# One-hots times gates moved from GpSimd to VectorE, and the next tile's query work dealt out over the placement batches

## The chip, the cores and the metric

One core of a Trainium2 chip runs the program alone. The metric is the device time of one execution in microseconds. Before the change three runs gave 3329.55, 3333.01 and 3342.83 us, median 3333.01.

## What is computed

One layer of a streaming encoder for 1024 prompt tokens and 8 x 16 sample tokens, so 9 tiles of 128 tokens with 1024 features. Two mixers and a projection come first; then each token asks for experts, and this is where the change lies:

```python
q = (h @ wq).reshape(N, 8, 2, 128)
s = einsum('nhpc,hpkc->nhpk', q, keys)          # 128 keys per head and half
sv, si = top_k(s, 16)                           # 16 best of 128, twice per head
cv, ci = top_k(sv[:, :, 0, :, None] + sv[:, :, 1, None, :], 16)   # 16 best pairs
expert = i1 * 128 + i2                          # the two keys of each pair
gate = softmax(cv)
a = gelu(einsum('nd,nhkd->nhk', h, u[expert]))
out = einsum('nhk,nhkd->nd', gate * a, v[expert])
```

Each token has 8 heads x 16 = 128 slots, each with two keys (below 128) and a gate. There are 16384 experts.

## The kernel before, in words

The program has four stages: modulation, mixing, routing, experts. Four of the nine tiles fetch the rows of their experts one by one ("picked" tiles); the other five are computed against the whole expert table ("dense" tiles), and for them the routing writes a matrix of gates per token, 128 x 128 keys, to memory. The change touches `routing` alone.

**Periods.** `periods` (L764) goes over the tiles in the order 0, 1, 4, 5, 6, 7, 8, 2, 3 (L761). Each engine runs the same sequence of periods, each with three parts for three tiles: *choose* (VectorE's search for the best keys of a tile), *done* (the tile chosen before it is indexed if it is picked, or placed if it is dense) and *prepare* (query product and scores of the tile that comes next). Periods 3 to 7 place the five dense tiles; 0, 1, 2 and 8 place nothing. In period 1 VectorE also does 32 dot products for tile 0 (`use`, L1088), whose rows GpSimd fetches (`fetch`, L830).

**Placement** of a tile goes in 16 batches of 8 tokens. For each, VectorE compares the slots' keys with a counter and makes two one-hots of 128 slots by 128 keys by 8 tokens in bf16 (`hot_rows`, L1105: left_hot L1113, right_hot L1116, stored with the 8 tokens innermost). ScalarE turns left_hot into f32 `left`, token by token (`left_rows`, L904). GpSimd multiplies right_hot by the gate into f32 `right`, also token by token (`place` on GpSimd, L839, instruction L846). TensorE multiplies right by left for each token (`place`, L1192), and ScalarE copies the result into `dense` (`take_gates`, L911). SP stores half a tile at a time (`store`, L802) behind its load of a coming tile's h2T (`load_h2`, L797), which waits for that query product's end. All of left_hot, right_hot, left and right have two buffers: one-hots of batch b wait for the reader of batch b - 2, right and left wait for the placement of batch b - 2 (`wait_for_placed`, L757).

**Query work** of VectorE for one tile: `two_lists` (L968) takes 16 maxima of 8, 16 pairs of index and replace, 16 maxima, 16 indices; `best_pairs` (L996) the same over the sums; `chosen_ranks` (L1029) the arithmetic on ranks, the product of hit with key_wide twice (L1066, L1070) and the sums; `softmax` (L1095) the gates. `own.settle()` waits for all of VectorE's own results so far; the call `rows(b)` ahead of most of them puts batch b of the placement there, so that the wait is filled. `rows(0)` stands behind the 16 pairs of index and replace. ScalarE makes key_wide (`widen_keys`, L893) and the exponential.

**Preparation** on TensorE: `product` (L1153) is one of four column blocks of the query product, 8 steps each (two matmul records per step); ScalarE copies it (`take_q`, L866), TensorE turns it (`turn`, L1171), ScalarE copies that (`take_qT`, L872), and `scores` (L1174) follows. In a period TensorE does product 0 first, then turns the slots of the tile done (`turn_slots`, L1182, which waits for the gates), product 1 with a turn in it, and then per batch the placement and two steps of products 2 and 3.

Which batch issues what is written out by hand in the engines' `period` functions; all engines run in program order.

Of the kernel before, what the change touches and what calls it, by code (L numbers as in the profile page):

```python
# [8 lines left out]
ALU = mybir.AluOpType  # L9
# [3 lines left out]
P = 128  # L13
D = 1024
KD = D // P
# [12 lines left out]
NKEYS = 128  # L28
# [669 lines left out]
def routing(nc, ctx, wq, keys, u_table, v_table, ident_in, shared, h2_rows, h2T_tiles, gate_blocks, picks):  # L698
# [12 lines left out]
    with ExitStack() as mem:  # L711
# [59 lines left out]

        def picks_rows(n):

            return ORDER[n] < PICKED
# [49 lines left out]
        def _(pool):  # L824
# [14 lines left out]
            def place(t):  # L839

                d = t - FIRST_DENSE
                pool.wait_ge(S.slotsT, t * 2 + 2)
                for b in range(BATCHES):
                    wait_for_placed(pool, d, b)
                    pool.wait_ge(S.right_hot, d * BATCHES + b + 1)
                    nc.gpsimd.tensor_tensor(  # L846
                        right[b % 2][:, :, :], right_hot[b % 2][:, :, :].rearrange("p i t -> p t i"),
                        gateT[:, b * BATCH:(b + 1) * BATCH].rearrange("p (t o) -> p t o", o=1)
                        .to_broadcast([P, BATCH, NKEYS]), ALU.mult).then_inc(S.right, 1)

            def period(choose, done, prepare):
                indexed, placed = split(done)
                if placed is not None:
                    place(placed)
# [3 lines left out]
            periods(period)  # L858

        @block.scalar  # L860
        def _(act):
# [59 lines left out]
            def period(choose, done, prepare):  # L921
                indexed, placed = split(done)
                if prepare is not None:
                    take_q(prepare, 0)
# [4 lines left out]
                if prepare is not None:  # L929
                    take_qT(prepare, 0)  # L930
                    take_q(prepare, 1)
                for b in range(BATCHES):
# [4 lines left out]
                    if prepare is not None and b in (4, 8):  # L937
                        take_q(prepare, b // 4 + 1)
                    if prepare is not None and b in (1, 5, 9):
                        take_qT(prepare, b // 4 + 1)  # L940
                    if choose is not None and b == 6:
                        widen_keys(choose, 0)
                    if choose is not None and b == 12:
                        act.wait_ge(S.shifted, choose + 1)
                        nc.scalar.activation(soft[:, :, :], soft[:, :, :], ACT.Exp).then_inc(S.exp, 1)
                    if choose is not None and b == 14:
                        widen_keys(choose, 1)
# [8 lines left out]
        def _(dve):  # L956
# [11 lines left out]
            def two_lists(t, rows):  # L968

                for n in range(HP):  # L970
# [3 lines left out]
                    own.mark(nc.vector.max(best[:, n, low], s_ps[:, n, :]))  # L974
                own.settle()
# [4 lines left out]
                rows(0)  # L980
# [4 lines left out]
                rows(1)  # L985
# [4 lines left out]
                rows(2)  # L990
# [3 lines left out]
                rows(3)  # L994
# [1016 lines left out]
```

## Time and profile before

| what | us |
|---|---|
| median of three runs | 3333.01 |
| profiled execution | 3337.24 |
| its span | 3335.6 |
| TensorE matmul busy | 3045.6 (91%) |
| VectorE busy | 2407.0 (72%) |
| GpSimd busy | 1489.0 (45%) |
| ScalarE busy | 935.2 (28%) |
| routing, from the first to the last of its query work | 512.6 to 1183.6 |
| placement, first left_hot to last dense copy | 724.8 to 1138.5 |

The span is the time from the first to the last instruction of the one profiled execution. Busy shares are means over stages that are bound by different engines; the routing stage is a fifth of the span and is read for itself. In the rows further down, PE is TensorE, DVE VectorE, ACT ScalarE, POOL GpSimd; L numbers are lines of the kernel; a group's row has the output and inputs, the shapes, the number of instructions, the busy time, the mean ns of one, and the idle time of the engine before them with what ended it. `work` is the memory of both the sums and hit; the names `shared` and `wq_sb` are the query weights.

### The profile page before, as it was taken

The page shows a single profiled execution, that of the slowest core. Times are in us where ns is not written, and L with a number is a line of the kernel's source. Part 1 is how long each engine was busy: PE and PEld are TensorE (multiplying, and loading weights), DVE is VectorE, ACT ScalarE, POOL GpSimd, SP SyncE. Part 2 cuts the span into 40 slices and gives each one's busy share as a digit, 9 for nine tenths or more (in the row PEclk, how much of TensorE's full clock was granted, in tenths as well). Part 3 has the DMA queues.
Part 4 walks back from the last instruction along what each step waited for, and adds up shares of the span by engine and source line. Part 5 has one row for each costly group of instructions (what it writes and reads, how often), then busy time and mean ns, then how long its engine had stood idle before and what let it go on. Part 6 is the DMA issues. An engine that isn't in the chain of part 4 may idle for free.

```text
span 3335.6 us, 43974 instructions
## 1 busy us (share of the span) xinstructions
PE 3045.6 (91%) x16658; PEld 2331.2 (70%) x16658; DVE 2407.0 (72%) x4987; ACT 935.2 (28%) x1271; POOL 1489.0 (45%) x1188
## 2 busy tenths in 40 slices
PE   8899978577888469999999999999999999999997
PEld 1466644245555369988888887888888888788886
DVE  1233324999988878887777777878777777778798
ACT  0111111138888622222222222222122222212222
POOL 0010000425554334346656565656565565666453
PEclk9999989889999879999999999999999999999999
DMA  9711131602222367789999999999999999999883
GB/s 357 212 64 63 57 145 64 208 7 108 108 108 108 151 223 264 265 292 353 366 351 366 359 350 368 353 370 353 355 351 369 349 360 344 352 347 336 307 295 140
DMA packets 305919, 858.73 MB, mean 257 GB/s; under 512 B 25376, under 2 KB 108832, under 8 KB 303984
## 3 DMA queue, kind: packets, MB, share of 16 engines
q0 software_dynamic: 151344, 551.09, 45.1%
q1 hardware_dynamic: 154333, 305.79, 25.6%
q8 instruction: 64, 1.05, 0.1%
q14 instruction: 70, 0.57, 0.1%
q10 hardware_dynamic: 108, 0.22, 0.0%
HBM read 793.86 MB, written 63.15 MB: 257 GB/s over the span
## 4 chain that ended last, share of the span: by engine, by line
PE 50%; DMA 5%; POOL 4%; DVE 3%; issue 2%; ACT 0%; DVEq 0%; SPq 0%; ACTq 0%
PE y_ps L1889 22%; PE a_ps L1870 20%; PE picked_ps L1907 5%; DMA shared<-in_peer_u,ids 3%; PE uT_ps L1857 3%; POOL shared L1453 2%; POOL quad L1464 1%; DMA shared<-in_peer_v,ids 1%; DVE uT_lo L1615 1%; DVE shared L1674 1%; DVE shared L1644 0%; DMA quad<-in_peer_v,idsT 0%; DVE shared L1657 0%; ACT uT_hi L1534 0%; DVE m_lo L1630 0%
## 5 line engine op out<-in xcount | busy, mean ns | idle before, releaser
L1453 POOL DMA_INDIRECT shared<-in_peer_u,ids x480 | 560.7, 1168 | 595.3 <-DVE acts L1657 507.1
L1657 DVE CUSTOM_DVE_ANT_0 shared<-shared 128x1024 f32<-128x1024 f32 x480 | 579.2, 1221 | 173.5 <-DMA shared<-in_peer_u,ids 172.9
L1870 PE MATMUL a_ps<-h_hi,uT_lo 128*128 128x320 f32 x2048 | 643.8, 314 | 1.7 <-DVE h_lo L1786 1.7
L1870 PE MATMUL a_ps<-h_hi,uT_hi 128*128 128x320 f32 x2048 | 633.8, 309 | 0.0
L1870 PE MATMUL a_ps<-h_lo,uT_hi 128*128 128x320 f32 x2048 | 633.8, 309 | 0.0
L1889 PE MATMUL y_ps<-v_hi,m_lo 128*128 128x512 f32 x1280 | 511.5, 400 | 25.7 <-DVE shared L1644 14.6
L1644 DVE TENSOR_TENSOR shared<-shared,y_ps 128x512 f32<-128x512 f32 x630 | 422.5, 685 | 150.2 <-PE y_ps L1889 149.5
L1889 PE MATMUL y_ps<-v_lo,m_hi 128*128 128x512 f32 x1280 | 504.6, 394 | 0.0
L1889 PE MATMUL y_ps<-v_hi,m_hi 128*128 128x512 f32 x1280 | 502.3, 392 | 0.0
L1464 POOL DMA_INDIRECT quad<-in_peer_v,idsT x384 | 443.9, 1156 | 120.1 <-issue 120.1
L1870 PEld LDWEIGHTS a_ps<-h_hi,uT_lo 128*128 128x128 f32 x2048 | 386.1, 189 | 7.2 <-issue 2.1
L1870 PEld LDWEIGHTS a_ps<-h_lo,uT_hi 128*128 128x128 f32 x2048 | 386.2, 189 | 4.9
L1870 PEld LDWEIGHTS a_ps<-h_hi,uT_hi 128*128 128x128 f32 x2048 | 385.5, 188 | 0.0
L1543 ACT ACTIVATE m_all<-a_ps 128x320 f32<-128x320 f32 x256 | 112.1, 438 | 918.2 <-PE a_ps L1870 918.2
L846 POOL TENSOR_TENSOR right<-right_hot,gateT 128x1024 f32<-128x1024 bf16 x80 | 215.6, 2698 | 264.6 <-DVE right_hot L1116 203.0
L1889 PEld LDWEIGHTS y_ps<-v_hi,m_lo 128*128 128x128 f32 x1280 | 241.2, 188 | 117.0 <-issue 33.6
L1889 PEld LDWEIGHTS y_ps<-v_hi,m_hi 128*128 128x128 f32 x1280 | 241.7, 189 | 53.9
L1534 ACT ACTIVATE uT_hi<-uT_ps 128x512 fp32r<-128x512 f32 x254 | 138.0, 596 | 488.7 <-PE uT_ps L1857 488.7
L1889 PEld LDWEIGHTS y_ps<-v_lo,m_hi 128*128 128x128 f32 x1280 | 241.8, 189 | 40.3
L1200 PE MATMUL place_ps<-left,right 128*128 128x128 f32 x1280 | 171.6, 290 | 87.8 <-ACT dense L918 64.8
L1200 PEld LDWEIGHTS place_ps<-left,right 128*128 128x128 f32 x1280 | 158.7, 202 | 120.9 <-issue 107.0
L1453 POOL DMA_INDIRECT shared<-in_peer_v,ids x128 | 154.2, 1205 | 186.8 <-DVE shared L1674 155.2
(187 smaller groups left out, 4197.2 us busy)
## 6 DMA issues: line engine op xcount, KB each, us to landing
shared<-in_peer_u SPq DMA_DIRECT2D x128, 512.0 KB, 7.5
v_all<-in_peer_v SPq DMA_DIRECT2D x128, 512.0 KB, 7.5
gate_blocks<-dense SPq DMA_DIRECT2D x10, 4096.0 KB, 12.1
gates<-gate_blocks SPq DMA_DIRECT2D x64, 640.0 KB, 22.1
w_ada<-in_w_ada SPq DMA_DIRECT2D x12, 2048.0 KB, 11.7
x_in<-in_x_prompt SPq DMA_DIRECT2D x16, 512.0 KB, 4.5
shared<-in_peer_u,ids POOLq DMA_INDIRECT x480, 8.7
shared<-in_w_in SPq DMA_DIRECT2D x8, 768.0 KB, 13.2
```

The source lines that it names most:

```text
L846: nc.gpsimd.tensor_tensor(right[b % 2][:, :, :], right_hot[b % 2][:, :, :].rearrange("p i t -> p t i"), gateT[:, b * BATCH:(b + 1) * BATCH ...
L1200: last = nc.tensor.matmul(place_ps[:, g, j, :], right[b % 2][:, g * 4 + j, :], left[b % 2][:, g * 4 + j, :], start=True, stop=True)
L1453: pool.indirect_dma_start(out=rows[n % 4], out_offset=None, in_=u_table if n < DOTS else v_table, in_offset=bass.IndirectOffsetOnAxis(ap=i ...
L1464: pool.indirect_dma_start(out=quads[half][q], out_offset=None, in_=v_table, in_offset=bass.IndirectOffsetOnAxis(ap=idsT[:, t, token:token ...
L1534: nc.scalar.activation(uT_hi[s][:, n * 4:n * 4 + 4, :], uT_ps[:, n * 4:n * 4 + 4, :], ACT.Copy)\
L1543: nc.scalar.activation(m_all[j][parity][:, n * GROUP:(n + 1) * GROUP], a_ps[n][:, 0:GROUP], ACT.Gelu).then_inc(S.gelu, 1)
L1644: nc.vector.tensor_tensor(part, part, y_ps[n % RING][:, :], ALU.add).then_inc(S.y_free, 1)
L1657: nc.vector.tensor_tensor_reduce(out=rows[n % 4], in0=rows[n % 4], in1=token_row, scale=1.0, scalar=0.0, op0=ALU.mult, op1=ALU.add, accum_ ...
L1857: last = nc.tensor.transpose(uT_ps[:, k, :], u[s][:, k * P:(k + 1) * P], ident[:, :])
L1870: last = nc.tensor.matmul(a_ps[n][:, 0:GROUP], lhs[s][:, k, :], rhs[:, k, tok], start=k == 0 and m == 0, stop=k == KD - 1 and m == 2)
L1889: last = nc.tensor.matmul(y_ps[n % RING][:, :], lhs[j][parity][:, tok], rhs[j][parity][:, col], start=j == 0 and m == 0, stop=j == 1 and m ...
L1907: last = nc.tensor.matmul(picked_ps[n][q * 32:(q + 1) * 32, :], spread[:, half, q, :], quads[half][q][:, n * HALF:(n + 1) * HALF], start=o ...
```

## The change

- GpSimd's placement loop goes. VectorE multiplies right_hot by the gate itself, in `hot_rows`, behind a wait for its own right_hot and for the placement of the batch before last.
- The calls of `rows` move: batch 0 behind the first 16 maxima, batches 1 to 5 among the 16 pairs of index and replace, batch 6 in the middle of the second maxima, 7 to 9 among the indices, 10 to 15 at the waits of `best_pairs` and `chosen_ranks`; none later.
- TensorE turns the slots first, and deals the four products out over batches 0 to 11 (3, 3 and 2 steps each), with turns in batches 4, 7, 10, 13 and scores in 9, 10, 12, 15. ScalarE's copies follow (`take_q` in 2, 5, 8, 11, `take_qT` in 5, 8, 11, 14), key_wide in 11 and 15.

```diff
+        QUERY_ENDS, SCORED = (2, 5, 8, 11), (9, 10, 12, 15)
...
-            def place(t):
-
-                d = t - FIRST_DENSE
-                pool.wait_ge(S.slotsT, t * 2 + 2)
-                for b in range(BATCHES):
-                    wait_for_placed(pool, d, b)
-                    pool.wait_ge(S.right_hot, d * BATCHES + b + 1)
-                    nc.gpsimd.tensor_tensor(
-                        right[b % 2][:, :, :], right_hot[b % 2][:, :, :].rearrange("p i t -> p t i"),
-                        gateT[:, b * BATCH:(b + 1) * BATCH].rearrange("p (t o) -> p t o", o=1)
-                        .to_broadcast([P, BATCH, NKEYS]), ALU.mult).then_inc(S.right, 1)
...
-            periods(period)
...
@@ ScalarE, period @@
-                if prepare is not None:
-                    take_q(prepare, 0)
                 if indexed is not None:
                     take_index(indexed)
                 if placed is not None:
                     take_slots(placed)
-                if prepare is not None:
-                    take_qT(prepare, 0)
-                    take_q(prepare, 1)
                 for b in range(BATCHES):
...
-                    if prepare is not None and b in (4, 8):
-                        take_q(prepare, b // 4 + 1)
-                    if prepare is not None and b in (1, 5, 9):
-                        take_qT(prepare, b // 4 + 1)
-                    if choose is not None and b == 6:
+                    if prepare is not None and b in QUERY_ENDS:
+                        take_q(prepare, QUERY_ENDS.index(b))
+                    if prepare is not None and b - 3 in QUERY_ENDS:
+                        take_qT(prepare, QUERY_ENDS.index(b - 3))
+                    if choose is not None and b == 11:
                         widen_keys(choose, 0)
-                    if choose is not None and b == 12:
+                    if choose is not None and b == 15:
                         act.wait_ge(S.shifted, choose + 1)
                         nc.scalar.activation(soft[:, :, :], soft[:, :, :], ACT.Exp).then_inc(S.exp, 1)
-                    if choose is not None and b == 14:
                         widen_keys(choose, 1)
@@ VectorE, two_lists @@
                     own.mark(nc.vector.max(best[:, n, low], s_ps[:, n, :]))
+                rows(0)
                 own.settle()
...
-                rows(0)
+                    if n % 3 == 2:
+                        rows(1 + n // 3)
                 own.settle()
...
@@ VectorE, hot_rows @@
-                wait(dve, S.right, d * BATCHES + max(b - 1, 0))
+                if b > 1 or d:
+                    dve.wait_ge(S.right, d * BATCHES + b - 1)
                 nc.vector.tensor_tensor(right_hot[b % 2][:, :, :], key(1), keys_iota, ALU.is_equal)\
                     .then_inc(S.right_hot, 1)
+                wait_for_placed(dve, d, b)
+                dve.wait_ge(S.right_hot, d * BATCHES + b + 1)
+                nc.vector.tensor_tensor(
+                    right[b % 2][:, :, :], right_hot[b % 2][:, :, :].rearrange("p i t -> p t i"),
+                    gateT[:, b * BATCH:(b + 1) * BATCH].rearrange("p (t o) -> p t o", o=1)
+                    .to_broadcast([P, BATCH, NKEYS]), ALU.mult).then_inc(S.right, 1)
@@ TensorE, period @@
-                if prepare is not None:
-                    product(prepare, 0)
                 if done is not None:
                     turn_slots(done)
-                if prepare is not None:
-                    product(prepare, 1, range(0, 5))
-                    if done is not None:
-                        pe.wait_ge(S.slotsT, done * 2 + 2)
-                    turn(prepare, 0)
-                    product(prepare, 1, range(5, KD))
                 for b in range(BATCHES):
                     if placed is not None:
                         place(placed - FIRST_DENSE, b)
-                    if prepare is not None:
-                        if b < 8:
-                            product(prepare, 2 + b // 4, range(b % 4 * 2, b % 4 * 2 + 2))
-                        if b in (0, 4, 8):
-                            turn(prepare, b // 4 + 1)
-                        if b in range(9, 13):
-                            scores(prepare, b - 9)
+                    if prepare is None:
+                        continue
+                    if b - 2 in QUERY_ENDS:
+                        if b - 2 == QUERY_ENDS[0] and done is not None:
+                            pe.wait_ge(S.slotsT, done * 2 + 2)
+                        turn(prepare, QUERY_ENDS.index(b - 2))
+                    if b <= QUERY_ENDS[-1]:
+                        product(prepare, b // 3, range(b % 3 * 3, min(b % 3 * 3 + 3, KD)))
+                    if b in SCORED:
+                        scores(prepare, SCORED.index(b))
```

## Rows read from the trace of the kernel before

**Rows 1.** table of windows: the period without placement, the five with it (busy us)

```profile
core 0: us, PE busy (x) PEld busy (x) DVE busy (x) ACT busy (x) POOL busy (x), PEclk, DMA share, GB/s
668.30:712.90 44.60, 35.55 (x114) 17.89 (x114) 40.74 (x219) 9.13 (x13) 0.00 (x0) 0.92 0.04 12
712.80:1138.30 425.50, 335.15 (x1839) 240.82 (x1839) 382.03 (x1249) 345.01 (x304) 215.64 (x80) 0.96 0.26 104
```

**Rows 2.** timeline of VectorE: the first maxima of three queries (start, duration, us)

```profile
668.34 3.26 DVE L974 MAX8 best<-s_ps 128x8 f32<-128x128 f32 x16
712.85 0.29 DVE L974 MAX8 best<-s_ps 128x8 f32<-128x128 f32 x1
1138.28 0.49 DVE L974 MAX8 best<-s_ps 128x8 f32<-128x128 f32 x2
```

**Rows 3.** groups by line, VectorE, 712.8 to 1138.3 (busy us, mean ns, idle before)

```profile
L1113 DVE TENSOR_TENSOR left_hot<-keyT,iota_keys 128x1024 bf16<-128x1024 bf16 x80 | 113.1, 1414 | 32.0 <-ACT left L908 31.9
L1116 DVE TENSOR_TENSOR right_hot<-keyT,iota_keys 128x1024 bf16<-128x1024 bf16 x80 | 65.5, 819 | 2.3 <-POOL right L846 2.3
L1066 DVE TENSOR_TENSOR work<-work,key_wide 128x2048 bf16<-128x2048 bf16 x5 | 16.7, 3344 | 0.2
L1070 DVE TENSOR_TENSOR work<-work,key_wide 128x2048 bf16<-128x2048 bf16 x5 | 11.2, 2240 | 6.8 <-ACT key_wide L900 6.8
```

**Rows 4.** groups by line, ScalarE, 712.8 to 1138.3

```profile
L908 ACT ACTIVATE left<-left_hot 128x1024 f32<-128x1024 bf16 x80 | 171.6, 2150 | 4.6 <-DVE left_hot L1113 4.6
L918 ACT ACTIVATE dense<-place_ps 128x512 f32<-128x512 f32 x160 | 163.3, 1152 | 8.1 <-PE place_ps L1200 8.0
```

**Rows 5.** timeline of VectorE: the first batch's one-hots, GpSimd idle

```profile
724.75 0.68 DVE L1113 TENSOR_TENSOR left_hot<-keyT,iota_keys 128x1024 bf16<-128x1024 bf16 x1
725.35 0.68 DVE L1116 TENSOR_TENSOR right_hot<-keyT,iota_keys 128x1024 bf16<-128x1024 bf16 x1
```

**Rows 6.** timeline of VectorE in the period without placement

```profile
700.54 0.43 DVE L1041 TENSOR_TENSOR ranks<-digits 128x256 f32<-128x256 uint32 x1
701.00 0.42 DVE L1044 TENSOR_TENSOR ranks<-ranks,narrow 128x256 f32<-128x256 f32 x1
707.97 1.22 DVE L1070 TENSOR_TENSOR work<-work,key_wide 128x2048 bf16<-128x2048 bf16 x1 [2.04 <-ACT key_wide L900]
```

**Rows 7.** groups by line, shapes apart, whole span: operands in order or broadcast

```profile
L546 DVE TENSOR_TENSOR x_in<-x_in,gated_mix 128x1024 f32<-128x1024 f32 x9 | 11.0, 1226 | 0.7
L412 ACT ACTIVATE squares<-x_in 128x1024 bf16<-128x1024 f32 x9 | 9.4, 1049 | 119.2 <-DMA x_in<-in_x_prompt 119.2
L1003 DVE TENSOR_TENSOR work<-best 128x512 f32<-128x512 f32 x9 | 6.2, 685 | 0.0
```

**Rows 8.** timeline of TensorE: second placement period, and the first placement of all

```profile
836.27 2.00 PE L1200 MATMUL place_ps<-left,right 128*128 128x128 f32 x16
838.11 1.88 PE L1162 MATMUL q_ps<-wq_sb,h2T 128*128 128x512 f32 x4
728.66 3.75 PE L1200 MATMUL place_ps<-left,right 128*128 128x128 f32 x16 [6.24 <-issue]
```

**Rows 9.** timeline of ScalarE, VectorE and TensorE in the periods 0 and 2

```profile
580.19 0.60 ACT L870 ACTIVATE q<-q_ps 128x512 f32<-128x512 f32 x1 [2.76 <-PE q_ps L1162]
581.33 3.74 PE L1179 MATMUL s_ps<-keysT,qT 128*128 128x128 f32 x32
582.18 1.22 DVE L1066 TENSOR_TENSOR work<-work,key_wide 128x2048 bf16<-128x2048 bf16 x1
694.43 0.60 ACT L870 ACTIVATE q<-q_ps 128x512 f32<-128x512 f32 x1 [2.76 <-PE q_ps L1162]
```

**Rows 10.** timeline at the start of period 1; landing times of line 834

```profile
591.05 3.26 DVE L974 MAX8 best<-s_ps 128x8 f32<-128x128 f32 x16
590.66 1.04 POOL L834 DMA_INDIRECT dense<-in_peer_u,ids  x1 [88.29 <-DVE ids L1085]
DMA to landing us min/median/max: 4.3/5.8/8.2
```

More of the change, by code:

```diff
@@ L837, in fetch @@
                     .then_inc(row_loaded[slot % 8], 16)
-            def place(t):
-                d = t - FIRST_DENSE
-                pool.wait_ge(S.slotsT, t * 2 + 2)
-                for b in range(BATCHES):
-                    wait_for_placed(pool, d, b)
-                    pool.wait_ge(S.right_hot, d * BATCHES + b + 1)
-                    nc.gpsimd.tensor_tensor(
-                        right[b % 2][:, :, :], right_hot[b % 2][:, :, :].rearrange("p i t -> p t i"),
-                        gateT[:, b * BATCH:(b + 1) * BATCH].rearrange("p (t o) -> p t o", o=1)
-                        .to_broadcast([P, BATCH, NKEYS]), ALU.mult).then_inc(S.right, 1)
[L851 to L854, printed above, removed]
             pool.wait_ge(S.picked, 1)
@@ L984, in two_lists @@
                     own.mark(nc.vector.max(best[:, n, high], work3[:, n, :]))
-                rows(1)
+                    if n == 7:
+                        rows(6)
                 own.settle()
@@ L989, in two_lists @@
                     own.mark(nc.vector.max_index(best_at[:, n, high], best[:, n, high], work3[:, n, :]))
-                rows(2)
+                    if n in (3, 9, 15):
+                        rows(7 + n // 6)
                 own.settle()
@@ L993, in two_lists @@
                 nc.vector.tensor_copy(best_key[:, :, :], best_at[:, :, :]).then_inc(S.best_key, 1)
-                rows(3)
             def best_pairs(t, rows):
@@ L1007, in best_pairs @@
                         ALU.add))
-                rows(4)
                 own.settle()
@@ L1013, in best_pairs @@
                         own.mark(nc.vector.max(pair[:, h, part], sums[:, h]))
-                    rows(5 + n * 3)
+                    rows(10 if part is low else 13)
                     own.settle()
@@ L1018, in best_pairs @@
                         own.mark(nc.vector.max_index(pair_at[:, h, part], pair[:, h, part], sums[:, h]))
-                    rows(6 + n * 3)
+                    rows(11 if part is low else 14)
                     own.settle()
@@ L1024, in best_pairs @@
                             own.mark(nc.vector.match_replace(sums[:, h], pair[:, h, low], sums[:, h], NEG))
-                        rows(7)
+                        rows(12)
                         own.settle()
@@ L1038, in chosen_ranks @@
                 own.mark(nc.vector.tensor_scalar(narrow[:, :, :], pair_at[:, :, :], NW, None, ALU.is_ge))
-                rows(10)
+                rows(15)
                 own.settle()
                 own.mark(nc.vector.tensor_tensor(ranks[:, :], digits[:, 2:4], digits[:, 0:2], ALU.subtract))
-                rows(11)
                 own.settle()
@@ L1046, in chosen_ranks @@
                     .to_broadcast([P, 2, HEADS, TOPK]), ALU.mult))
-                rows(12)
                 own.settle()
                 own.mark(nc.vector.tensor_tensor(ranks[:, :], ranks[:, :], digits[:, 0:2], ALU.add))
-                rows(13)
                 own.settle()
@@ L1055, in chosen_ranks @@
                 own.mark(nc.vector.tensor_copy(rank[:, 1], ranks[:, 1]))
-                rows(14)
                 own.settle()
@@ L1067, in chosen_ranks @@
                     .then_inc(S.first_keyed, 1)
-                rows(15)
                 dve.wait_ge(S.key_wide, t * 2 + 2)
```

## The prediction, made before the changed kernel was run

> **What bounds the kernel now.** I read the page's engine shares and its chain of waits first. The chain is TensorE's in the expert stage, and nothing of the change lies there, so the question is one stage only: the routing, whose placement periods are read with the table of windows [rows 1]. Five periods place a dense tile each; from the first maximum of one query to that of the next they last 425.4 us together (712.85 to 1138.28), 85.1 us each [rows 2]. One period without placement, the query of one tile alone, lasts 44.5 us (668.34 to 712.85) [rows 2]. Everything after the routing waits for it, so what a period gains or loses goes into the total one to one.
>
> In the placement window VectorE is busy 382 of 425.5 us, 90%; ScalarE 345, TensorE 335, GpSimd 216 [rows 1]. The reader should see that GpSimd, the engine that the change empties, has the most room, and VectorE, which gets its work, the least. VectorE's own idle time is mostly left_hot waiting for ScalarE, 31.9 us [rows 3]. So the first half of a period is VectorE's and the second ScalarE's: there it does left and two dense copies per batch, 171.6 + 163.3 us for 80 batches, 4.2 us each by the records, which overlap a little [rows 4].
>
> The row that argues for the change: left_hot takes 0.68 us where GpSimd is idle [rows 5] but 1.41 us in the mean, right_hot 0.82, and the two multiplications of hit by key_wide, of one form, 3.34 and 2.24 us in these periods [rows 3] against 1.22 without GpSimd [rows 6]. GpSimd's multiplication slows VectorE.
>
> **The change part by part.**
>
> *Removed.* 80 multiplications, 216 us in all [rows 1], leave GpSimd. They had no time of their own on the path, since VectorE and ScalarE set it. What returns is VectorE's: 80 x (1.41 - 0.68) + 80 x (0.82 - 0.68) + 5 x (3.34 - 1.22) + 5 x (2.24 - 1.22) = 58 + 11 + 11 + 5 = 85 us of busy time; some of it was hidden behind the wait for ScalarE.
>
> *Added.* 80 multiplications on VectorE, 128x1024, f32 out. The trace shows none with this operand order: right_hot is stored key by key with the 8 tokens innermost and is read token by token, so each bf16 element lies 16 bytes from the one before it. Bounds: below, the f32 product of 128x1024 with operands in order, 1.23 us [rows 7]; 0.68 us, right_hot's own time with bf16 in and out, would need the speed of bf16, and I hold it unlikely because gate and output are f32. Above, ScalarE's pair of rows: 1.05 us for 128x1024 in order [rows 7], 2.15 us for left [rows 4], the very same turned read of a one-hot; the ratio 2.05 on 1.23 gives 2.5 us. The broadcast gate costs nothing (sums of two broadcast operands, 128x512, 0.685 us [rows 7], about half of 1.23). I take the nearest row, ScalarE's turned read, and its extra 1.0 to 1.1 us as a time rather than a ratio, rounded down: m = 2.2 us.
>
> One batch on VectorE is then left_hot 0.60 (start to start [rows 5]), right_hot 0.68, a wait on its own result of 0.03 (an operation that waits starts 0.03 us behind the end of its producer, 700.97 to 701.00 [rows 6]), and m less the 0.08 us by which the next starts early: 3.43 us. Behind the new waits (own result, placement of the batch before last) stands the whole query chain of the next tile.
>
> *Moved query work on VectorE.* The hot rows go to other places between the same instructions; the count stays 16. Eight of the groups still stand directly ahead of a wait for VectorE's own results and fill it. A bare wait costs some 0.2 us (0.03 behind the end in place of 0.08 to 0.09 before it, plus the lost overlap of the short ones), so the chain of 44.5 us loses 8 x 0.2 = 1.6 us.
>
> *A placement period after the change:* 44.5 - 1.6 + 16 x 3.43 = 97.8 us if VectorE is never held up, against 85.1: +12.7 us, five times +63.5 us. The way of summing holds for the kernel before: the same sum with its rows, 44.5 + 16 x (1.41 + 0.82 - 0.16) + 3.1 for the hit products + 34/5 of waits for left and right [rows 3] - 16 x 0.2, gives 84.3 where 85.1 was measured.
>
> *What must keep up.* ScalarE has 345/5 = 69 us of work per period, 98 us to do it in. TensorE's new batch holds three steps of a query product in place of two: place 1.84 us (836.27 to 838.11), steps of 0.86 (two of them, four records of 0.43 us, in the 1.88 us row with its last overlap taken off), so 4.4 us, with a turn 4.9 [rows 8]; VectorE's batch in the first third, with three pairs of index and replace at 0.53 us (16 of them between the maxima's 3.4 us behind 712.85 and left_hot at 724.75 [rows 2, 5]), is 3.43 + 1.6 = 5.0. It just keeps up, and two buffers of right and left take the rest. Turning the slots ahead of the first product frees the tile edge, and rows(0) goes out right behind the 3.26 us of maxima [rows 2], not 8.5 us later. That spread is a gain for ScalarE and TensorE, and I cost it at nothing because VectorE's chain covers it.
>
> *Moved queue work.* No DMA is added. SP's load of h2T waits for the last product, now in batch 11 instead of 7; it and the store of half a tile queued behind it have four batches of some 5 us and the tail of the query as cover, so nothing; without the cover each period would lose what reaches past its end. GpSimd's queue keeps only its early fetches.
>
> *Periods without placement*, where the new order costs. Period 0: two of the four groups of scores (3.74 us in all, so 1 each) now come before the last product's end, so ScalarE's last take_q moves from 580.19 to 582.2; the first key_wide, about 1.9 us (VectorE waits 2.04 for the second [rows 6]), now queues behind it and is done at 584.6, where VectorE wants it at 582.18: 2.4, and with the exponential that also queues behind it +3 us [rows 9]. Period 1: rows(0) moves to 3.3 us behind the first maximum at 591.05, but the first row was asked for at 590.66 and takes 4.3 to 8.2 us: +3 [rows 10]. Period 2: TensorE does all four products in the period, not three: 16 records of 0.43 us and a wait of 0.7 more, so with the scores the last take_q moves from 694.43 to 704.0, and key_wide is done at 706.4, where VectorE wants it at 704.7 (707.97 less the wait and one product): +2 [rows 6, 9]. Together +8 us, between 0 and 16.
>
> **Sum.** The profiled execution took 3337.2 us, its span 3335.6; 63.5 + 8 = +72 makes 3409. The median of the three runs shown is 4.2 us below it, so 3405.
>
> **Rivals.**
> 1. *The turned read costs VectorE only part of what it costs ScalarE.* For: nothing in the rows ties the two engines; ScalarE's slope may be its own. With half of the extra, m = 1.75, a batch is 2.98 and a period 90.6: 5 x 5.5 + 8 = +36, 3369. It decides by m alone; 0.25.
> The Trainium skill's Vector Engine (DVE) Microarchitecture Reference, section 5.2 (Measured stream behaviour on trn2), says that a port streams at full rate only over runs of at least two adjacent words, and gives 1.73 ns per column where one source hops at every element. An estimate from that is 1.8 us plus some 0.15 fixed, m = 1.9, and 3381 us. No run here shows it yet; it speaks against the change as my row does.
> 2. *The turned read is free on VectorE* (the other side). m = 1.23: a batch 2.46, a period 82.2, -14.5 + 8 = -6, 3327. For: no row shows VectorE paying for such a read. Against: ScalarE pays for the very same one. It decides below m = 1.5, where the total comes within 17 us; 0.11.
> 3. *Faster*: m near 1.0 or less, so that ScalarE's 69 us and the query's tail bound a period at about 78: -27, 3306; 0.07. Against: VectorE's f32 rows.
> 4. *TensorE becomes the bound.* It now idles from the last place to the next, some 20 us per tile, and after 6.2 us of idle time 16 place records took 3.75 us, not 2.00 [rows 8]. If the first twelve batches ran at such a rate (8.2 us each), a period would be about 120 us and the total 3510. Against: one batch later the records are at the quick pace again, as the table's mean over the placement shows (clock 0.96 [rows 1]); 0.02.
>
> **How the numbers follow.** My forecast (m between 1.9 and 2.5, 3381 to 3429) has 0.55, rival 1 has 0.25, rivals 2 to 4 have 0.11, 0.07 and 0.02. Slower by over 0.5% (17 us, about what a measurement can tell here) 0.82, same 0.11, faster 0.07. The range takes in the forecast and rival 1 with the bounds of m and of the periods without placement: low 3355 (m = 1.65 and nothing lost there), high 3445 (m = 2.5, twice the 8 us and as much again of waits not foreseen).
>
> **What would show it.** Multiplications on VectorE, 80 of about 2.2 us; left_hot and right_hot at 0.68 throughout; both hit products at 1.22; periods of 98 us between first maxima; VectorE over 95% busy in the placement window, with ScalarE and TensorE waiting for right and left_hot, not the reverse. I am wrong if the multiplication is near 1.23, or if periods are longer than the sum of VectorE's rows, which would put the wait on place or left.

## The result, and the profile after

The changed kernel takes 3466.88 us (median of 4 runs, 3460.10 to 3468.73), the kernel before 3337.18 (4 runs): ratio 1.0386, 95% interval [1.0358, 1.0415]. It is slower, as forecast, but by 130 us where the working said 72, and outside the range. The profiled execution took 3467.91 us, 130.7 more than that of before.

Where the time went is read first from the first maxima of each query, the rows that answer to [rows 2]. VectorE's timeline of the changed kernel, at the period without placement, the first placed one and the last (start, duration, us):

```profile
531.57 0.89 DVE L953 MAX8 best<-s_ps 128x8 f32<-128x128 f32 x4 [41.72 <-PE s_ps L1162]
596.72 3.25 DVE L953 MAX8 best<-s_ps 128x8 f32<-128x128 f32 x16
...
678.65 1.47 DVE L953 MAX8 best<-s_ps 128x8 f32<-128x128 f32 x7
...
725.36 0.89 DVE L953 MAX8 best<-s_ps 128x8 f32<-128x128 f32 x4
...
1266.52 0.69 DVE L953 MAX8 best<-s_ps 128x8 f32<-128x128 f32 x3
```

The five placed periods last 541.2 us (725.36 to 1266.52), 108.2 each, against 425.4 before: +115.7. Periods 0 to 2 last 65.15, 81.93 and 46.71 us where they had been 61.90, 77.29 and 44.51: +10.1. The first maximum comes 2.4 us later and what stands behind the placement takes 2.4 us longer. That is the whole 130.7, to the rounding. My sum had 63.5 and 8 for the first two, so 52 of the 58 us that are missing lie in the placed periods.

The table of windows over that stretch, answering to [rows 1] (busy us and instructions of each engine, granted clock, DMA share):

```profile
678.65:725.30 46.65, 36.00 (x114) 17.98 (x114) 40.55 (x218) 8.69 (x13) 0.00 (x0) 0.94 0.04 12
725.30:1266.60 541.30, 374.48 (x1855) 280.45 (x1855) 457.00 (x1329) 346.47 (x305) 0.00 (x0) 0.82 0.21 85
```

GpSimd's column is empty, as the change says. VectorE is busy 457 of 541 us, 84%, where it had been 90% before and over 95% was forecast. So VectorE has 75 us more work and is waiting more, and no other engine is near full. TensorE needs 374 us for the work that took 335, at a granted clock of 0.82 in place of 0.96. The groups by line of VectorE in the same stretch (busy us, mean ns, idle before and what ended it), answering to [rows 3, 5]:

```profile
L1097 DVE TENSOR_TENSOR right<-right_hot,gateT 128x1024 f32<-128x1024 bf16 x80 | 160.7, 2009 | 57.2 <-PE place_ps L1183 50.7 <-DVE right_hot L1093 1.4
L1093 DVE TENSOR_TENSOR right_hot<-keyT,iota_keys 128x1024 bf16<-128x1024 bf16 x80 | 54.8, 685 | 0.0
L1089 DVE TENSOR_TENSOR left_hot<-keyT,iota_keys 128x1024 bf16<-128x1024 bf16 x80 | 54.2, 678 | 12.9 <-ACT left L893 12.9
...
L1046 DVE TENSOR_TENSOR work<-work,key_wide 128x2048 bf16<-128x2048 bf16 x5 | 6.1, 1225 | 10.2 <-ACT key_wide L885 10.2
L1043 DVE TENSOR_TENSOR work<-work,key_wide 128x2048 bf16<-128x2048 bf16 x5 | 6.1, 1224 | 0.2
```

The right-hand numbers are the news: 57.2 us in which the multiplication waits, 50.7 of them for TensorE's placement, and 12.9 in which left_hot waits for ScalarE: 14 us a period. Who holds up TensorE stands in the waits of the same stretch (us in total, times, longest):

```profile
ACT q L855 <- PE q_ps L1145: 104.4, 20, 6.3
PE place_ps L1183 <- ACT dense L903: 102.1, 29, 5.9
...
DVE right L1097 <- PE place_ps L1183: 50.7, 27, 3.5
```

TensorE waits for ScalarE's dense copies 102 us, ScalarE for TensorE's query product 104 us, 20 times: once for each product. The same two lines before the change:

```profile
PE place_ps L1200 <- ACT dense L918: 64.8, 47, 3.5
...
ACT q L870 <- PE q_ps L1162: 37.2, 11, 6.9
```

TensorE waited for dense before, too, but in many short gaps; ScalarE waited for q in 11, not 20. That the two engines now wait for each other in a loop is seen in the timeline of the second placed period. TensorE:

```profile
870.02 1.95 PE L1183 MATMUL place_ps<-left,right 128*128 128x128 f32 x16
871.81 1.88 PE L1145 MATMUL q_ps<-shared,h2T 128*128 128x512 f32 x4
877.79 3.75 PE L1183 MATMUL place_ps<-left,right 128*128 128x128 f32 x16 [4.10 <-ACT dense L903]
881.33 3.70 PE L1145 MATMUL q_ps<-shared,h2T 128*128 128x512 f32 x6
884.87 1.95 PE L1183 MATMUL place_ps<-left,right 128*128 128x128 f32 x16
```

ScalarE over the same stretch:

```profile
873.73 0.60 ACT L855 ACTIVATE q<-q_ps 128x512 f32<-128x512 f32 x1 [5.44 <-PE q_ps L1145]
874.22 0.59 ACT L860 ACTIVATE qT<-x_ps 128x512 f32<-128x512 f32 x1
874.70 2.02 ACT L893 ACTIVATE left<-left_hot 128x1024 f32<-128x1024 bf16 x1
876.61 1.92 ACT L903 ACTIVATE dense<-place_ps 128x512 f32<-128x512 f32 x2
```

Read the two together. ScalarE has finished left and the copies of the batch before, and `take_q` is next in its queue. It waits 5.44 us, because TensorE ends that product only behind the placement of the same batch (870.02) and two more steps (871.81 to 873.69). What TensorE needs for its next placement, left of the next batch and the first dense copy of this one (which frees the half of place_ps), stands behind `take_q` in ScalarE's queue. So the two engines take turns: TensorE idles 4.10 us. Then it pays again: the next 16 records of the placement take 3.75 us where the others take 1.95. (The 20 such gaps of the five periods last 3.6 to 5.9 us, and the 16 records behind each take 3.4 to 3.8.) The windows around it (same columns as above) show the clock:

```profile
870.00:874.00 4.00, 3.69 (x21) 2.36 (x19) 3.86 (x18) 0.27 (x1) 0.00 (x0) 1.00 0.00 0
874.00:878.00 4.00, 0.21 (x1) 0.24 (x2) 3.90 (x12) 4.00 (x5) 0.00 (x0) 0.80 0.00 0
878.00:882.00 4.00, 4.00 (x17) 3.67 (x18) 2.19 (x8) 3.68 (x4) 0.00 (x0) 0.50 0.00 0
...
886.00:890.00 4.00, 4.00 (x22) 2.56 (x20) 3.49 (x5) 1.93 (x2) 0.00 (x0) 1.00 0.01 4
```

The granted clock goes from 1.00 (2.4 GHz) to 0.50 (1.2 GHz) in the stretch that follows the idle one, and is at 1.00 again in the window from 886 on. VectorE feels it when a `right` that needs the buffer of that batch waits for the late placement:

```profile
881.58 2.00 DVE L1097 TENSOR_TENSOR right<-right_hot,gateT 128x1024 f32<-128x1024 bf16 x1 [1.81 <-PE place_ps L1183]
```

The same picture stands at 893.37 and 913.54 (waits of 5.44 and 6.30 us), in all in batches 2, 5, 8 and 11 of every placed period.

### The profile page after: what moved, and what is told of

Same layout as the page of the kernel before. It is cut to its first block, busy times and chain, and to the rows that moved or that the text cites. A ratio compares the mean times of both kernels' runs of the same rounds, so it can differ in the third digit from the quotient of the medians.

```text
span 3466.3 us, 43971 instructions
## 1 busy us (share of the span) xinstructions
PE 3084.3 (89%) x16658; PEld 2370.6 (68%) x16658; DVE 2483.2 (72%) x5067; ACT 934.5 (27%) x1271; POOL 1271.0 (37%) x1108
## 4 chain that ended last, share of the span: by engine, by line
PE 49%; DMA 5%; POOL 3%; DVE 3%; issue 2%; ACT 0%; DVEq 0%; SPq 0%; ACTq 0%
PE y_ps L1867 22%; PE a_ps L1848 20%; PE picked_ps L1885 4%; DMA shared<-in_peer_u,ids 3%; PE uT_ps L1835 3%; POOL shared L1431 2%; POOL quad L1442 1%; DMA shared<-in_peer_v,ids 1%; DVE uT_lo L1593 1%; DVE shared L1652 0%; DVE shared L1622 0%; DVE shared L1635 0%; ACT uT_hi L1512 0%; DMA quad<-in_peer_v,idsT 0%; DVE m_all L1603 0%
## 5 line engine op out<-in xcount | busy, mean ns | idle before, releaser
L1867 PE MATMUL y_ps<-v_hi,m_lo 128*128 128x512 f32 x1280 | 512.7, 401 | 26.5 <-DVE shared L1622 14.3
L1183 PE MATMUL place_ps<-left,right 128*128 128x128 f32 x1280 | 200.9, 323 | 129.7 <-ACT dense L903 102.1
L1183 PEld LDWEIGHTS place_ps<-left,right 128*128 128x128 f32 x1280 | 192.2, 235 | 163.7 <-issue 133.9
## 6 DMA issues: line engine op xcount, KB each, us to landing
gate_blocks<-dense SPq DMA_DIRECT2D x10, 4096.0 KB, 12.9
```

Source lines behind the costliest of these rows:

```text
L1183: last = nc.tensor.matmul(place_ps[:, g, j, :], right[b % 2][:, g * 4 + j, :], left[b % 2][:, g * 4 + j, :], start=True, stop=True)
L1867: last = nc.tensor.matmul(y_ps[n % RING][:, :], lhs[j][parity][:, tok], rhs[j][parity][:, col], start=j == 0 and m == 0, stop=j == 1 and m ...
```

## The experiments

Periods are from first maximum to first maximum; a placed period is the mean of the five. Each ratio is to runs of the kernel before on the same chip; its median was 3335.65 us over the 25 of them that stand beside e5 to e8.

| run | multiplies | query work | placed period | us | ratio, 95% interval |
|---|---|---|---|---|---|
| before | GpSimd | old order | 85.1 | 3337.18 | 1 |
| after | VectorE | spread | 108.2 | 3466.88 | 1.0386 [1.0358, 1.0415] |
| e1 | VectorE | spread, q one batch later | 96.0 | 3397.21 | 1.0189 [1.0162, 1.0215] |
| e2 | GpSimd | spread | 106.5 | 3460.33 | 1.0371 [1.0349, 1.0393] |
| e3 | VectorE | old order | 92.9 | 3373.22 | 1.0116 [1.0094, 1.0139] |
| e4 | VectorE, read in stored order | as e1 | 83.5 | 3337.59 | 1.0001 [0.9988, 1.0014] |
| e5 | GpSimd | as e1 | 81.7 | 3327.34 | 0.9970 [0.9960, 0.9980] |
| e6 | VectorE, 8 tensor_scalar | as e1 | 85.2 | 3345.29 | 1.0027 [1.0016, 1.0038] |
| e7 | VectorE, 8 tensor_scalar | old order | 84.5 | 3337.32 | 1.0003 [0.9993, 1.0014] |
| e8 | VectorE | as e1 in two of four places | 101.3 | 3426.84 | 1.0265 [1.0248, 1.0282] |
| e9 | GpSimd | as e5; old order where nothing is placed | 82.2 | 3326.61 | 0.9962 [0.9946, 0.9977] |
| e10 | GpSimd | as e9, key_wide ahead of the last q | 81.9 | 3321.05 | 0.9945 [0.9930, 0.9961] |

**e1: the copy of q one batch later.** Only ScalarE's order changes:

```diff
-                    if prepare is not None and b in QUERY_ENDS:
-                        take_q(prepare, QUERY_ENDS.index(b))
+                    if prepare is not None and b - 1 in QUERY_ENDS:
+                        take_q(prepare, QUERY_ENDS.index(b - 1))
```

> The changed kernel, but ScalarE copies each finished query product one batch later (batches 3, 6, 9, 12 in place of 2, 5, 8, 11), behind left and the dense copies of that batch. Theory A (ScalarE stands at take_q until TensorE, behind the placement of the same batch, has ended the product, and left and the dense copies queue behind it): the idle time of ScalarE before take_q in the placement window falls from 120 us to under 30, VectorE's waits for the placement from 51 us to under 15, and a placement period from 108.2 us to VectorE's sum of 95 to 98 (44.5 - 1.6 + 16 x 3.23 = 94.6 and a few us of waits), so 3395 to 3415 us. Rival B (three product steps per batch are too much for TensorE, whatever ScalarE does): periods stay above 104 us and the total above 3440. Rival C (the price is the multiplication alone): unchanged, 3460 to 3470.

Measured: 3397.21 us, placed periods of 96.0. The waits for q are gone, and ScalarE now waits for VectorE, as the prediction had wanted it. Groups of ScalarE, then of VectorE, over the five placed periods of e1:

```profile
L893 ACT ACTIVATE left<-left_hot 128x1024 f32<-128x1024 bf16 x80 | 165.6, 2070 | 88.8 <-DVE left_hot L1089 88.8
...
L855 ACT ACTIVATE q<-q_ps 128x512 f32<-128x512 f32 x20 | 12.9, 643 | 0.0
```

```profile
L1097 DVE TENSOR_TENSOR right<-right_hot,gateT 128x1024 f32<-128x1024 bf16 x80 | 160.9, 2011 | 9.3 <-DVE right_hot L1093 1.4
```

The window of the five placed periods of e1 (columns as above):

```profile
720.47:1200.49 480.02, 349.64 (x1855) 253.89 (x1855) 456.56 (x1328) 349.10 (x305) 0.00 (x0) 0.88 0.24 96
```

VectorE is busy 95% of the time here, as the prediction had expected of the changed kernel. Idle time ahead of `right` and left_hot falls from 70.1 to 9.3 us, 12.2 a period, and the period falls by just that, 108.2 to 96.0. Moving one instruction by one batch gives 70 us back, 61 of them in the placed periods, so the queue order is shown to be the cause of the excess, not the multiplication's price (it is the same 2.01 us) nor GpSimd's absence.

**e8: the same in two places of four.**

```diff
-                    if prepare is not None and b in QUERY_ENDS:
+                    if prepare is not None and b in (3, 6):
+                        take_q(prepare, b // 3 - 1)
+                    if prepare is not None and b in (8, 11):
                         take_q(prepare, QUERY_ENDS.index(b))
```

> The changed kernel with only the first two of the four take_q moved one batch later. If each take_q is a stall of its own, half of the difference between the changed kernel (108.2 us per period) and e1 (96.0) comes back: 102 us, 3425 to 3440 us. If one stall is enough to hold up the whole period, 3455 or more.

Measured: 3426.84 us, periods of 101.3, near the middle of 108.2 and 96.0, and 10 waits for q (46.8 us) where there had been 20. Each early copy is a stall of its own, worth some 3 us of the period.

**e2 and e3: one part of the change each.** e2 is the changed kernel with GpSimd's loop put back (and the multiplication taken out of `hot_rows`); e3 is the kernel before with that loop taken out and the multiplication put into `hot_rows`, and nothing moved:

```diff
@@ e2, against the kernel after; e3 is the reverse, against the kernel before @@
+            def place(t):
...
+                    nc.gpsimd.tensor_tensor(
...
-                nc.vector.tensor_tensor(
-                    right[b % 2][:, :, :], right_hot[b % 2][:, :, :].rearrange("p i t -> p t i"),
```

> The changed kernel with the multiplication given back to GpSimd as it was; the dealing out of the query work and the places of the hot rows stay as changed. Theory A: four times per period ScalarE's wait for the product and TensorE's wait for left and the dense copies follow each other, about 7.6 us from one placement to the next instead of 4.4 (4 x 7.6 + 12 x 4.4 = 83, and some 10 us at the tile edge), so periods of 90 to 97 us although nothing was added to VectorE, and a total of 3370 to 3410 us, slower than before. Rival C (the multiplication on VectorE is the whole loss): as before or faster, 3340 us or less.

> The kernel before with the multiplication alone moved to VectorE; the query work and the hot rows stay where they were. Theory A: VectorE's chain sets the period, 44.5 - 3.2 + 16 x 3.23 = 93.0 us in place of 85.1, without the 10 us that the periods without placement lost: 3337 + 40 = 3377, between 3365 and 3395 us. Rival D (VectorE's new wait for the placement is what costs): periods above 100 us and 3420 us or more.

e3 came as forecast: 3373.22 us, placed periods of 92.9, and the three periods without placement at 61.84, 77.30 and 44.53, as before. e2 was a miss: the spread alone, with VectorE relieved of the multiplication, still costs 124 us (0.0371 x 3337), with periods of 106.5. I had taken the stall to be cheap where VectorE has time to spare. It isn't: VectorE is busy only 353 of e2's 532.5 us, and the period is nearly that of the kernel after, so the loop of ScalarE and TensorE holds it up by itself (e5 below takes the loop out). The waits of e2:

```profile
POOL right L848 <- PE place_ps L1194: 240.9, 62, 9.0
...
DVE left_hot L1106 <- ACT left L910: 164.6, 40, 12.5
...
ACT q L872 <- PE q_ps L1156: 110.9, 20, 6.3
PE place_ps L1194 <- ACT dense L920: 101.8, 29, 5.9
```

The last two are the pair of the kernel after, to within 7 us; GpSimd waits for the placement and VectorE for left. So the parts don't add: the spread costs 21.4 us a period with GpSimd multiplying, the multiplication 7.8 in the old order, both together 23.1. In the kernel after, the multiplication that I had priced at nearly the whole loss is all but hidden behind the loop: 108.2 against 106.5.

**e5: GpSimd multiplies, q one batch later.** e2 with the edit of e1.

> GpSimd multiplies as in the kernel before, the query work is spread as changed, and take_q comes one batch later. If the spread of the change cost only through take_q, its loss goes: VectorE's sum with GpSimd's disturbance is 44.5 - 1.6 + 16 x 2.07 + 3.1 = 79 us per period, so 79 to 84 us where the kernel before has 85.1, and with the 10 us of the periods without placement 3315 to 3345 us. If the spread costs by itself (TensorE's longer batches), periods stay above 90 us and the total above 3365.

Measured: 3327.34 us, ratio 0.9970: below both kernels, though by 0.3% only against the one before. With GpSimd multiplying, the copy one batch later takes the placed period from 106.5 to 81.7, so the early copy alone costs 24.8 us a period there. With the copy in its place the spread is a gain of 3.4 us a period, though periods 0 to 2 lose 6.8 us together. And e1 against e5 is the price of the multiplication on VectorE once the loop is out: 96.0 against 81.7, 14.3 us a period, 70 us in the total.

**e4: what the turned read costs.** e1, with right_hot read in the order in which it is stored; the gates of the dense tiles then land at other keys.

```diff
-                    right[b % 2][:, :, :], right_hot[b % 2][:, :, :].rearrange("p i t -> p t i"),
+                    right[b % 2][:, :, :], right_hot[b % 2][:, :, :].rearrange("p (t j) u -> p t (j u)", t=BATCH),
```

> As e1_q_later, but the multiplication reads right_hot in the order in which it is stored, so the one-hots times gates land at the wrong keys (the gates of the dense tiles are wrong, the work is the same). If the turned read is what makes the multiplication 2.0 us, it takes 1.2 us here; the period falls by 16 x 0.8 = 12 us against e1_q_later to 82 to 87 us (ScalarE's and TensorE's 69 us do not bound it) and the total by about 60, to 3330 to 3360. If the f32 output or the broadcast gate makes it 2.0 us, nothing changes against e1_q_later.

The group of the multiplication in e4, over its five placed periods:

```profile
L1097 DVE TENSOR_TENSOR right<-right_hot,gateT 128x1024 f32<-128x1024 bf16 x80 | 98.0, 1226 | 9.3 <-DVE right_hot L1093 0.9 <-PE place_ps L1183 0.5
```

1226 ns, to the nanosecond the f32 product in order of [rows 7], against 2011: the stride costs 0.785 us of each, 80 x 0.785 = 63 us, and the total falls by 60. This is the measured price of the operand order by itself.

**e6 and e7: no right_hot, no turned read.** Each token's row of `right` is made by one instruction from its key and gate, eight per batch; e6 on e1, e7 on the kernel before.

```diff
...
-                nc.vector.tensor_tensor(right_hot[b % 2][:, :, :], key(1), keys_iota, ALU.is_equal)\
-                    .then_inc(S.right_hot, 1)
...
+                for t in range(BATCH):
+                    tok = b * BATCH + t
+                    last = nc.vector.tensor_scalar(right[b % 2][:, t, :], iota_row[:, :], gateT[:, 0, tok:tok + 1],
+                                                   gateT[:, 1, tok:tok + 1], ALU.is_equal, ALU.mult)
...
```

> take_q one batch later, and VectorE makes right in one pass per token: eight operations of 128x128 per batch compare a row counter with the token's key and multiply by its gate, both as scalars per partition, in place of right_hot and the turned multiplication (2.75 us per batch). A 128x128 operation with a constant took 0.16 us from start to start, so 1.24 us per batch: VectorE 44.5 - 1.6 + 16 x 1.84 = 72 us per period. Theory: ScalarE's 69 us with its own waits then share the bound, 75 to 82 us per period, 3295 to 3335 us, below both kernels. If scalars from memory make an operation 0.3 us or more, 90 us and more, 3370 or above.

> As e6, but with the order of the kernel before (query work and hot rows where they were). VectorE's sum is 44.5 - 3.2 + 16 x 1.84 = 71 us. If the spread is worth something once VectorE is lighter, this is slower than e6: the tile edge stays (slots turned behind a whole product, batch 0 behind the 16 pairs), 78 to 85 us per period, 3305 to 3338 us. If it is worth nothing, this beats e6 by the 10 us of the periods without placement.

e6 missed: 3345.29 us. Eight such instructions in a row take 2.14 us, 0.27 each, where I had expected 0.155. Timeline of VectorE in e6:

```profile
762.74 0.67 DVE L1091 TENSOR_TENSOR left_hot<-keyT,iota_keys 128x1024 bf16<-128x1024 bf16 x1
763.33 2.14 DVE L1096 TENSOR_SCALAR right<-iota_row,gateT 128x128 f32<-128x128 f32 x8
```

That is more than `right` alone had cost, though right_hot (0.68) falls away. e7 lands at 3337.32, 1.0003 [0.9993, 1.0014]: taking the work off GpSimd in this way gains nothing that can be told from no change. It is 8 us below e6, as its expectation had it for a spread that is worth nothing. Most of that is the periods 0 to 2, 7.2 us together; a placed period is 0.7 us shorter. With the turned multiplication, e3 with its periods of 92.9 is below e1 with 96.0. So once q is copied late, the old order is no worse for a VectorE that multiplies, and better by 3.1 us a period with the dearer multiplication. That fits its groups of work, which stand ahead of more of the waits for VectorE's own results, but the two orders differ in more than that, and it wasn't tried apart.

**e9 and e10: the periods without placement.** e9 is e5 with the old order of TensorE, ScalarE and the dot products wherever no tile is placed; but key_wide stood behind the last copy of q. e10 puts it ahead:

```diff
@@ e10, against e9 @@
-                    for b in range(4 if prepare is not None else 0):
-                        take_qT(prepare, b)
-                        if b < 3:
+                    for b in range(4):
+                        if prepare is not None:
+                            take_qT(prepare, b)
+                        if choose is not None and b == 2:
+                            widen_keys(choose, 0)
+                        if prepare is not None and b < 3:
                             take_q(prepare, b + 1)
                     if choose is not None:
-                        widen_keys(choose, 0)
                         act.wait_ge(S.shifted, choose + 1)
```

> The kernel of the experiment with GpSimd's multiplication and the later copies of q, with the order of the kernel before in the periods that place no tile (0, 1, 2 and 8: query product, ScalarE's copies, and the places of the 32 dot products). If the new order is what cost the 10 us there (63.6, 82.3 and 44.6 us against 61.9, 77.3 and 44.5 from first maximum to first maximum, and 2.4 us ahead of the first), these three return to 62, 77 and 44.5, the placed periods stay at 81 to 82, and the total is 3317 us (3310 to 3325), ratio about 0.994. If instead the loss comes from code that is only longer or from the DMA's hour of the day (the rows fetched in period 1), the three periods stay as they are and the total stays at 3327.

> The kernel of the experiment before this one, with the first key_wide back ahead of the last copy of q in ScalarE's order, in the periods without placement, where the kernel before has it. There period 0 had stayed at 63.5 us, though its matmuls went in the old order, and key_wide ran at 586.30, behind the last copy of q at 584.46. If key_wide behind that copy is what costs period 0, it returns to 61.9 us here, with 77.3, 44.5 and 82 for the others; if not, it stays at 63.5. In the total this is 1.6 us, less than a comparison of runs can tell: 3325 us (3315 to 3332), ratio about 0.996.

In e9 periods 1 and 2 returned to 77.30 and 44.50, but period 0 stayed at 63.49. In e10 all three are those of before: 61.89, 77.31, 44.51. ScalarE in period 0, e9 and then e10:

```profile
584.46 0.60 ACT L872 ACTIVATE q<-q_ps 128x512 f32<-128x512 f32 x1 [4.56 <-PE q_ps L1193]
585.80 0.60 ACT L877 ACTIVATE qT<-x_ps 128x512 f32<-128x512 f32 x1 [0.75 <-PE x_ps L1202]
586.30 1.90 ACT L902 ACTIVATE key_wide<-best_key 128x2048 bf16<-128x2048 bf16 x1
```

```profile
579.16 1.90 ACT L902 ACTIVATE key_wide<-best_key 128x2048 bf16<-128x2048 bf16 x1
583.82 0.60 ACT L872 ACTIVATE q<-q_ps 128x512 f32<-128x512 f32 x1 [2.76 <-PE q_ps L1195]
```

So 1.6 us of period 0 are that one position. The total of e9 missed the expected 3317 us by 10: in its profiled run the first maximum came at 533.63 where e5 has 529.34, and period 0 did not return. e10 at 3321.05 is the fastest of all, 0.9945 [0.9930, 0.9961]; its interval overlaps with e9's, so between these two nothing is decided.

## Why the prediction was right in sign and wrong in size

- **The step that failed** is the paragraph on what must keep up: "ScalarE has 345/5 = 69 us of work per period, 98 us to do it in", and TensorE's batch of 4.4 to 4.9 us "just keeps up, and two buffers of right and left take the rest". Both sums of work are right (ScalarE is busy 346 us here) and both miss what the order does. I looked at what the waits of VectorE and SP's load would hold up, and didn't ask of the moved `take_q` what stands behind it in ScalarE's own queue. A product that ends behind the placement of batch 2, copied in batch 2, ahead of the copy that frees the placement's PSUM, closes a loop of TensorE and ScalarE, in which one waits while the other works. The second buffers of right and left don't open it: left of the next batch stands behind `take_q` in the same queue, and place_ps has one copy of each half. In the kernel before, product 2 ended in batch 3 and was copied in batch 4. Shown by e1 (12.2 us a period, 61 of 130 us), e8 (half of it) and e2 against e5 (24.8 us a period without the multiplication).
- **What the rest of the sum made.** Without the loop a placed period is 10.9 us longer than before (e1, 96.0 against 85.1), where 12.7 was forecast. So the 115.7 us of the placed periods are 61 of the loop, for which the sum had nothing, and 55 of the multiplication in the new order, for which it had 63.5. The sign is not luck: e1, without the loop, is still 60 us slower than the kernel before. The low end of the range was added up 3 us too high (m = 1.65 gives 3352), which changes nothing here.
- **The term m** was 2.2 us and measured 2.009 (the group of `right` above), inside its bounds of 1.23 and 2.5. From start to start a batch is left_hot 0.59, right_hot 0.78 (the wait for its own result is 0.10, not 0.03) and `right` 1.93, so 3.30 where I had 3.43. The same sum then gives 44.5 - 1.6 + 16 x 3.30 = 95.7 for a period that is never held up; e1 measured 96.0. The way of summing held, though the 1.6 was not measured by itself, and its answer was not the bound in the kernel after.
- **Rival 1** put m at 1.75, which was too low. The Trainium skill's Vector Engine (DVE) Microarchitecture Reference, section 5.2 (Measured stream behaviour on trn2), put it at an estimated 1.9. That estimate is 5% below the 2.009 us measured and was nearer than ScalarE's row, 10% above. The Trainium skill's 1.73 ns per column is for a source of 4-byte words that hops 4 KiB at every element; no row of it has one source of bf16 at a step of 16 bytes, so the agreement is no test of its rule. Rivals 2 and 3 needed m below 1.5 and are out.
- **What returns to VectorE** came as read: left_hot 0.678, right_hot 0.685, both hit products 1.224 and 1.225 us, against 1.41, 0.82, 3.34 and 2.24 with GpSimd at work [rows 3]. e5 shows the converse: left_hot at 1.43 again.
- **Rival 4**, TensorE as the bound through the low clock, had 0.02. Its mechanism is there, though as a consequence: 16 records in 3.4 to 3.8 us behind each stall, and a clock of 0.82 over the five periods. It doesn't start the loss, since in e1, with the same work, TensorE's waits for dense are 2.7 us at most and VectorE is the bound, though the clock is at 0.88, below the 0.96 of before. How much of the 12.2 us is waiting and how much the slow restart was not tried apart.
- **The periods without placement** cost 10.1 us where 8 were forecast. Period 2: 2.20 (forecast 2), by key_wide behind the last copy of q, which came 35.6 us behind the first maximum, and 35.7 was worked out; e1, where key_wide stands ahead of that copy again, gets 2.0 of it back. Period 0: 3.25 (forecast 3), of which that place of key_wide is only half. VectorE waits for both key_wide there:

```profile
587.42 1.23 DVE L1043 TENSOR_TENSOR work<-work,key_wide 128x2048 bf16<-128x2048 bf16 x1 [2.87 <-ACT key_wide L885]
591.25 1.23 DVE L1046 TENSOR_TENSOR work<-work,key_wide 128x2048 bf16<-128x2048 bf16 x1 [2.60 <-ACT key_wide L885]
```

e1 gets 1.6 back and still waits 3.83 us for the second, where 2.18 were waited before, because its last copy of q, with the exponential and the second key_wide behind it, comes 52.7 us behind the first maximum in place of 51.0. Period 1: 4.64 (forecast 3), but only 1.45 us are the fetched rows; another 2.0 is the wait for the second key_wide, which two dot products had filled before and which I had not charged there. The other 1.2 was not split. In e10, with the old order in these periods, all three are back.

- **What I said would show me wrong** did: periods longer than the sum of VectorE's rows, with the wait on place and left. It was named as a sign and given no chance of its own; as a rival it would have widened the range upward.

## What to carry to other kernels

When a step moves in an in-order queue, don't compare the engine's total work with the time; list what stands behind the moved instruction in that queue, and ask whether the engine that it waits for needs one of those for its own next step. Here a copy issued in the batch in which its product ends, rather than one batch later, cost 61 us on two engines that had a third of their time free. And where a change has two parts, price each alone and both together: here they cost 21.4, 7.8 and 23.1 us a period, and the half that looked cheap cost more by itself than the other.

## What the runs showed of the hardware that was not expected

- Reading bf16 with a step of 16 bytes takes VectorE 2.01 us for 128x1024 where 1.226 in stored order do (e4). The extra 0.785 us is less than the 1.0 to 1.1 between ScalarE's rows for the same turned read and for another operation in order [rows 4, 7].
- A 128x128 tensor_scalar in f32 with key and gate taken per partition runs at 0.27 us in a row of eight (e6), so eight small instructions cost more than the one turned one of 2.01.
- The first maximum of the routing came between 528.7 (e2) and 533.6 us (e9) in the profiled runs, of kernels whose program is alike up to there: the first product's 16 records took 7.13 us in the kernel before and 10.06 in the kernel after. So the 2.4 us by which it came later after the change belong to no edit that the runs show.
